# Moving projection tiles behind the block inversion, and re-ordering the queues beside it, in a two-block mixer kernel

## The reference

```python
h = rms_norm(x, pre_norm_w)
qkv, z, b_logit, a_logit = split(h @ w_in)
qkv = silu(causal_depthwise_conv(qkv, conv_w))        # 4 taps
q, k, v = split(qkv)                                  # 8 key heads, 16 value heads of 128
# per value head, in chunks: strictly lower A, (I + A)^-1 applied to v and k
a_mat = where(strict, (k * beta) @ k.T * decay, 0)
u = solve(I + a_mat, v * beta); w = solve(I + a_mat, k * beta * exp(g))
# scan over the chunks, state S
v_new = u - w @ S; o = q_dec @ S + qk @ v_new; S = S * sd + k_dec.T @ v_new
y = (rms_norm(o, norm_w) * silu(z)) @ w_out
...
# memory: the rows of mem are normed by themselves before the key and value projections
kv = rms_norm_2(mem, mem_norm_kv)
```

## Time and profile before

| | |
|---|---|
| median of 3 runs | 1812.25 us (1811.49 to 1813.73) |
| the profiled execution | 1811.49 us, span 1809.7 us |
| mean granted TensorE clock | 0.999 of full speed |
| TensorE busy | 1781.1 us, 98% |
| VectorE busy | 993.0 us, 55% |
| ScalarE busy | 721.1 us, 40% |
| GpSimd busy | 140.6 us, 8% |
| HBM traffic | 86 GB/s over the span |

### The profile page before, as it was taken

One profiled execution on the slowest core, in us unless ns is written; L12 is line 12 of the kernel. 1 busy time (PEld: TensorE's weight loads), 2 busy tenths in 40 slices (PEclk: granted clock), 3 DMA queues, 4 the chain that ended last, 5 costly groups with the idle time before them and its releaser, 6 DMA issues.

```text
span 1809.7 us, 26548 instructions
## 1 busy us (share of the span) xinstructions
PE 1781.1 (98%) x10563; PEld 1438.3 (79%) x10563; DVE 993.0 (55%) x1669; ACT 721.1 (40%) x1381; POOL 140.6 (8%) x108
## 2 busy tenths in 40 slices
PE   8999999999999999999999999999999999999998
PEld 6788888887887888888888777478876778888887
DVE  4645656466537544444443656744333687778434
ACT  5644656457445221111234623754123532223323
POOL 1113031221002000000000001610000100000000
PEclk9999999999999999999999999999999999999999
DMA  6422222122334322333223351023222222332221
GB/s 193 84 61 70 61 63 63 54 71 61 109 102 108 113 93 93 98 104 99 94 93 94 91 117 47 24 70 116 94 70 93 70 93 95 107 99 93 93 76 64
DMA packets 183183, 158.18 MB, mean 87 GB/s; under 512 B 36977, under 2 KB 179886, under 8 KB 183050
## 3 DMA queue, kind: packets, MB, share of 16 engines
q1 hardware_dynamic: 172672, 152.88, 27.6%
q0 software_dynamic: 1248, 3.19, 1.2%
q10 hardware_dynamic: 9163, 0.72, 0.4%
HBM read 152.77 MB, written 3.73 MB: 86 GB/s over the span
## 4 chain that ended last, share of the span: by engine, by line
PE 91%; DVE 4%; ACT 3%; issue 1%; DMA 1%; SPq 0%; POOL 0%; ACTq 0%; DVEq 0%
PE bank L740 13%; PE bank L742 13%; PE bank L741 13%; PE bank L841 5%; PE bank L842 5%; PE bank L843 5%; PE bank L940 4%; PE bank L942 4%; PE bank L941 4%; PE bank L730 4%; PE bank L1067 1%; PE bank L1078 1%; PE bank L1134 1%; PE bank L1089 1%; PE bank L1333 1%
## 5 line engine op out<-in xcount | busy, mean ns | idle before, releaser
L1520 ACT ACTIVATE w_hi<-ring 128x2048 fp32r<-128x2048 f32 x122 | 233.8, 1917 | 535.4 <-PE bank L742 376.3
L740 PE MATMUL bank<-h_hi,w_hi 128*128 128x512 f32 x1024 | 400.4, 391 | 2.2 <-DVE w_lo L2130 2.0
L742 PE MATMUL bank<-h_hi,w_lo 128*128 128x512 f32 x1024 | 398.5, 389 | 0.0
L741 PE MATMUL bank<-h_lo,w_hi 128*128 128x512 f32 x1024 | 398.4, 389 | 0.0
L2130 DVE TENSOR_TENSOR w_lo<-ring,w_hi 128x2048 fp32r<-128x2048 f32 x105 | 240.4, 2289 | 246.4 <-ACT w_hi L1520 246.4
L740 PEld LDWEIGHTS bank<-h_hi,w_hi 128*128 128x128 f32 x1024 | 192.2, 188 | 45.1 <-issue 3.8
L742 PEld LDWEIGHTS bank<-h_hi,w_lo 128*128 128x128 f32 x1024 | 192.2, 188 | 40.3
L741 PEld LDWEIGHTS bank<-h_lo,w_hi 128*128 128x128 f32 x1024 | 192.3, 188 | 39.9 <-issue 0.5
L841 PE MATMUL bank<-h_hi,w_hi 128*128 128x512 f32 x432 | 170.6, 395 | 1.8 <-DVE arena L2823 1.0
L843 PE MATMUL bank<-h_hi,w_lo 128*128 128x512 f32 x432 | 168.2, 389 | 0.0
L842 PE MATMUL bank<-h_lo,w_hi 128*128 128x512 f32 x432 | 168.2, 389 | 0.0
(11 more groups left out here) (441 smaller groups left out, 2508.6 us busy)
## 6 DMA issues: line engine op xcount, KB each, us to landing
ring<-in_sc_w_in SPq DMA_DIRECT2D x32, 1024.0 KB, 5.4
ring<-in_gdn_w_in SPq DMA_DIRECT2D x24, 1024.0 KB, 5.4
ring<-in_w_up SPq DMA_DIRECT2D x22, 1024.0 KB, 5.1
ring<-in_gdn_w_out SPq DMA_DIRECT2D x8, 1024.0 KB, 5.3
ring<-in_sc_w_out SPq DMA_DIRECT2D x8, 1024.0 KB, 5.2
ring<-in_w_down SPq DMA_DIRECT2D x8, 1024.0 KB, 5.3
ring<-in_w_in SPq DMA_DIRECT2D x4, 1024.0 KB, 5.6
ring<-in_w_mk SPq DMA_DIRECT2D x4, 1024.0 KB, 5.1
```

What stands on the lines that cost most here:

```text
L740: pe.matmul(o, a_hi(k), b_hi(k), start=(k == tiles[0]), stop=False)
L741: pe.matmul(o, a_hi(k), b_lo(k), start=False, stop=False)
L742: mm = pe.matmul(o, a_lo(k), b_hi(k), start=False, stop=(k == tiles[-1]))
L1520: act.activation(w_hi[:, plan[n]["pair"], :], ring[:, n % 2, :], ACT.Copy).then_inc(w_hi_ready, 1)
```

## The change

In the delta-rule layer: (a) TensorE's `next_group(1)` and `next_group(3)` ahead of the wait for the blocks go, and the scan's counts rise (first step 5, 5, 4 tiles and not 4, 4, 3; later steps 4, 4, 4 and not 4, 3, 3; in the last step 4 and 4 and not 3 and 3, and then the rest). (b) ScalarE does the squares and roots of the group before ahead of its block copies, and not behind them, and `split_hi(6g+6)` behind the key rows. (c) The low part of slab 6g+6 moves from VectorE, ahead of the inversion, to GpSimd, behind it. (d) `scaled_outs` in groups 1 to 3 moves from ScalarE to VectorE, in the place of that split; VectorE's version is the one that the last group used already. At the seam: (e) SP issues the load of the memory rows behind slab XOUT+1 and not XOUT+3, with the same wait. (f) The statistics of the rows move on ScalarE from ahead of `post_norm` to behind its chunk 0, and (g) their scaling on VectorE from ahead of it to behind the second addition.

```diff
--- before.py
+++ after.py
@@ -661,7 +661,7 @@
                              w_out_2[0, 256 * f:256 * f + 256, o].rearrange("(k d) c -> d k c", d=DH)) for f in range(2)]
                            + [(lambda r: r[:, 1024:SLOT].rearrange("p (k c) -> p k c", c=256),
                                w_out_2[0, 512:D, o].rearrange("(k p) c -> p k c", p=P))])
-                if n == 3:
+                if n == 1:
                     sp.wait_ge(attT_out, NT)
                     sp.dma_start(mem_rows, mem_2[0].rearrange("(t p) c -> p t c", p=P)).then_inc(mem_in, 16)
             load(w_mk_2[0].rearrange("(k p) c -> p k c", p=P)[:, :, 0:256], wide(256))
@@ -1030,6 +1030,12 @@
                     mm.then_inc(vt_done, 1)
                 project(10, range(2, KD))
                 project(11, range(KD))
+                if g:
+                    turn_outs(g - 1, v_of[(g + 1) % 2], banks_read=4 * g)
+                else:
+                    pe.wait_ge(vb_ready, 4)
+                    keep_clock(4, 10)
+                pe.wait_ge(blocks_moved, PER_GROUP * (g + 1))
                 next_tiles = iter([(n, k) for n in range(8) for k in range(KD)])
                 out_sides = iter([(pair, k, side) for pair in range(2) for k in range(KD) for side in range(2)])
 
@@ -1045,16 +1051,6 @@
                                 pe.wait_ge(q_summed, 8 * g + 8)
                             out_tile(VH, 0, pair, k, (side,))
 
-                if ahead:
-                    next_group(1)
-                if g:
-                    turn_outs(g - 1, v_of[(g + 1) % 2], banks_read=4 * g)
-                else:
-                    pe.wait_ge(vb_ready, 4)
-                    keep_clock(4, 10)
-                if ahead:
-                    next_group(3)
-                pe.wait_ge(blocks_moved, PER_GROUP * (g + 1))
                 for lv in range(DEEP):
                     n0 = 4 * (DEEP * g + lv)
                     for h in range(HG):
@@ -1125,7 +1121,7 @@
                             pe.matmul(psum[4 + h][:, 0:P], k_T[h // 2][:, i], state[:, h, :], start=True, stop=True)
                             pe.matmul(psum[4 + h][:, P:2 * P], q_T[h // 2][:, i], state[:, h, :], start=True, stop=True)\
                                 .then_inc(ks_done, 1)
-                    next_group((4 if c < NCH - 1 else 3) if ahead else 1)
+                    next_group((4 if c else 5) if ahead else 1)
                     for h in range(HG):
                         if c:
                             pe.wait_ge(resid_ready, HG * ((NCH - 1) * g + c - 1) + h + 1)
@@ -1133,14 +1129,14 @@
                             pe.wait_ge(y_ready, 4 * (DEEP * (g + 1) - 1) + h + 1)
                         pe.matmul(psum[4 + h][:, 0:P], Y_T[:, h, i], resid[:, h, :] if c else v_T[:, h, i], start=True, stop=True)\
                             .then_inc(vn_done, 1)
-                    next_group((3 if c else 4) if ahead else 1)
+                    next_group((4 if c else 5) if ahead else 1)
                     for h in range(HG):
                         pe.wait_ge(vn_ready, n0 + h + 1)
                         if c < NCH - 1:
                             pe.matmul(psum[4 + h][:, P:2 * P], k_rows[:, h // 2, i], v_dec[:, h, :], start=True, stop=True)
                         pe.matmul(psum[4 + h][:, 2 * P:3 * P], QK_T[:, h, i], v_new[:, h, :], start=True, stop=True)\
                             .then_inc(su_done, 1)
-                    next_group(64 if c == NCH - 1 else 3 if ahead else 2)
+                    next_group(64 if c == NCH - 1 else 4 if ahead else 2)
             turn_outs(GROUPS - 1, v_T)
 
             def x_tiles_back(parts):
@@ -1714,15 +1710,6 @@
                 own.settle()
                 act.activation(ssq[:, 1, :], ssq[:, 1, :], ACT.Exp, scale=-0.5).then_inc(l2_rms, 1)
 
-            def scaled_outs(g, v_T):
-
-                act.wait_ge(l2_rms, 2 * g + 2)
-                for h in range(HG):
-                    for t in range(NT):
-                        rows = v_T[:, h, t * P:(t + 1) * P]
-                        ins = act.activation(rows, rows, ACT.Copy, scale=ssq[:, 1, 4 * h + t:4 * h + t + 1])
-                    ins.then_inc(ssq_ready, 1)
-
             def query_sums(g, j):
                 act.wait_ge(q_turned, 2 * g + j + 1)
                 for t in range(NT):
@@ -1759,20 +1746,17 @@
                         ins = act.activation(decay(g, h)[:, t * P:(t + 1) * P], psum[4 + h][:, t * P:(t + 1) * P],
                                              ACT.Exp, bias=decay_bias(g)[:, t, h:h + 1])
                     ins.then_inc(decay_ready, 1)
+                if g:
+                    out_squares(g - 1, v_of[(g + 1) % 2], (NT - 1,))
+                    out_roots(g - 1)
                 for b in rows_of_scalar:
                     r = slice(BLK * b, BLK * b + BLK)
                     act.wait_ge(a_ready, HG * (g + 1))
                     act.dma_start(block_view(blocks_d, b), diagonal[0][r, :, r]).then_inc(blocks_moved, 16)
-                if g:
-                    out_squares(g - 1, v_of[(g + 1) % 2], (NT - 1,))
-                split_hi(6 * g + 6)
-                if g:
-                    out_roots(g - 1)
                 for j in range(2):
                     act.wait_ge(kr_done, 2 * g + j + 1)
                     act.activation(k_rows[:, j, :], psum[4 + 2 * j][:, :], ACT.Copy).then_inc(kr_ready, 1)
-                if g:
-                    scaled_outs(g - 1, v_of[(g + 1) % 2])
+                split_hi(6 * g + 6)
                 for n in range(8, 11):
                     projected(g, n)
                 for b in rows_of_scalar:
@@ -2006,16 +1990,16 @@
                     if what == "c":
                         out_columns(n)
 
-            act.wait_ge(mem_in, 16)
-            for t in range(MT):
-                own.did(act.activation(mem_junk, mem_rows[:, t, :], ACT.Square, accum_out=small[:, 1 + t:2 + t]))
-                own.settle()
-            own.did(act.activation(small[:, 1:3], small[:, 1:3], ACT.Ln, bias=eps, scale=1.0 / D))
-            own.settle()
-            act.activation(small[:, 1:3], small[:, 1:3], ACT.Exp, scale=-0.5).then_inc(mem_rstd, 1)
-
             def mem_beside(k):
 
+                if k == 0:
+                    act.wait_ge(mem_in, 16)
+                    for t in range(MT):
+                        own.did(act.activation(mem_junk, mem_rows[:, t, :], ACT.Square, accum_out=small[:, 1 + t:2 + t]))
+                        own.settle()
+                    own.did(act.activation(small[:, 1:3], small[:, 1:3], ACT.Ln, bias=eps, scale=1.0 / D))
+                    own.settle()
+                    act.activation(small[:, 1:3], small[:, 1:3], ACT.Exp, scale=-0.5).then_inc(mem_rstd, 1)
                 if 3 <= k < 7:
                     for j in (2 * k - 6, 2 * k - 5):
                         act.wait_ge(mem_turned, j + 1)
@@ -2426,7 +2410,7 @@
                     dve.tensor_tensor(QK_T[:, h, :], kq[:, h // 2, :], decay(g, h), ALU.mult).then_inc(decay_used, 1)
                 if g:
                     out_means(g - 1)
-                split_lo(6 * g + 6)
+                    scaled_outs(g - 1, v_of[(g + 1) % 2])
                 invert_blocks(g)
                 for h in range(HG):
                     dve.wait_ge(vt_done, 4 * g + turn_order.index(h) + 1)
@@ -2769,9 +2753,11 @@
                     if (what, s, n) == ("s", len(steps) - 1, 3):
                         shares(s, n)
 
-            dve.wait_ge(mem_rstd, 1)
-            own.did(dve.tensor_scalar(mem_rows[:, 0, :], mem_rows[:, 0, :], small[:, 1:2], None, ALU.mult))
-            dve.tensor_scalar(mem_rows[:, 1, :], mem_rows[:, 1, :], small[:, 2:3], None, ALU.mult).then_inc(mem_scaled, 1)
+            def mem_scale(k):
+                if k == 1:
+                    dve.wait_ge(mem_rstd, 1)
+                    own.did(dve.tensor_scalar(mem_rows[:, 0, :], mem_rows[:, 0, :], small[:, 1:2], None, ALU.mult))
+                    dve.tensor_scalar(mem_rows[:, 1, :], mem_rows[:, 1, :], small[:, 2:3], None, ALU.mult).then_inc(mem_scaled, 1)
 
             def split_q0(k):
                 if k == 5:
@@ -2779,7 +2765,7 @@
                     dve.tensor_tensor(w_lo[:, Q0["pair"], :], q0_slab, w_hi[:, Q0["pair"], :].bitcast(F32), ALU.subtract)\
                         .then_inc(split_ready, 1)
 
-            post_norm(between=split_q0, ahead=lambda pair: split_lo(XOUT + 2 + pair) if pair < 2 else None)
+            post_norm(beside=mem_scale, between=split_q0, ahead=lambda pair: split_lo(XOUT + 2 + pair) if pair < 2 else None)
             split_lo(MEM0 + 4)
             norm_ready()
             q0 = plan[MEM0 + 3]["end"] - 2
@@ -2877,6 +2863,7 @@
                     pool.wait_ge(vn_done, HG * NCH * g)
                 pool.memset(Y_T, 0.0).then_inc(y_cleared, 1)
                 pool.wait_ge(inverted, g + 1)
+                split_lo(6 * g + 6)
                 split_lo(6 * g + 7)
                 if g + 1 < GROUPS:
```

## The result

The changed kernel took 1830.71 us (median of 4 runs, 1828.8 to 1833.78), the kernel before, beside it on the same chip, 1812.47: a ratio of 1.0102, 95% interval 1.0089 to 1.0115. It is 18.2 us slower, and the forecast was 8.6. Its profiled execution took 1827.32 us with a span of 1825.5 and a mean granted clock of 0.996; ten runs of it, that one among them, had a mean clock of 0.9935.

The account below looks back on a forecast made before the run. TensorE, busy 98% of the span, bounds the kernel, so only its stalls count. Blocks +3.7, memory rows' stall +3.2 and clock +1.7 sum to +8.6 us; forecast 1820.9 us, its own range 1817 to 1823.

Parts of the forecast that it names:

- clock behind L1063: After the new stalls before L1067, some 2.3 us each: no clock drop, 0, with 5.1 us as upper bound.
- wait at the memory rows: At L1407 TensorE stands from 1216.15 to 1219.4 for VectorE's late scaling: +3.2 us, bounds 2.6 and 4.7.
- clock behind the memory rows: Behind the stall at L1407 the granted clock drops as it did behind L730: +1.7 us, bounds 0 and 1.7.
- signs of being right: L1067 waits 2 us or more, block copies 3 us late, last scan matmuls 1.05, L1407 waits 3 with a dip.
- the block chain's terms: Late inverted blocks at L1067, moved tiles and scan gain counted: -0.8, +1.7, +1.7, +1.1 in groups 0 to 3, +3.7 us.
- Part 1: Four tiles moved behind L1067: 2.7 us less cover there, 1.0 us won in the scan's last step, groups 0 to 2.
- Part 3: The split on GpSimd behind the inversion, 4.58 us against VectorE's 2.29: costs 0, and doesn't hold VectorE.
- Part 4: Memory rows at the seam: load not earlier, statistics and scaling late, TensorE stalls +3.2 us, clock drop behind it +1.7.
- the shorter chain: Rival at ScalarE's first block copy, groups 1 to 3: not late, L1067 waits for nothing, 1813 or 1808; chance 0.10.
- hidden memory edit: Rival at the memory rows: TensorE doesn't meet the late scaling, only the blocks' +3.7 stays, 1816; chance 0.10.
- GpSimd holding VectorE: Rival at VectorE's scaling of v: starts 4.6 us late in every group, +13 on the forecast, 1834; chance 0.06.
- The clock rival: Rival at L1067: the clock drops there too, one to three more drops of 1.7 us, 1822.6 to 1826.0; chance 0.14.

Follow-up runs that it names:

- e10: The changed kernel with the memory edit undone: 1826.35 us, 1.0072 of the kernel before.
- e11: The changed kernel with the memory edit undone and idle matmuls (8, 12, 7) in the stalls before L1063 of groups 1 to 3: 1821.74 us, ratio 1.0041.
- e9: The kernel before with only the four tiles moved behind L1067: 1817.65 us, ratio 1.0029.
- e13: The changed kernel as it is, measured again in a later session: 1828.37 us, 1.0089 of the kernel before.
- e3: The changed kernel with ScalarE's block copies again ahead of the squares and roots: 1818.47 us, 1.0028 of the kernel before.
- e8: The kernel before with the tiles moved and the split on GpSimd, but ScalarE's order, scaled outputs and memory rows as before: 1812.12 us, ratio 0.9998.
- e4: The changed kernel with the four tiles again ahead of L1063 and the old counts in the scan: 1834.27 us, 1.012 of the kernel before.
- e7: The kernel before with only ScalarE's squares and roots of the group before put ahead of its block copies: 1818.15 us, ratio 1.0028.
- e1: The kernel before with the memory edit alone: 1815.82 us, ratio 1.0019.
- e5: The changed kernel with idle matmuls (8, 12, 7) in the stalls before L1063 of groups 1 to 3: 1828.54 us, 1.0087 of the kernel before.
- e6: The changed kernel with tiles ahead of L1063, old scan counts, and the split on VectorE between scaled outputs and inversion: 1825.37 us, 1.0068 of the kernel before.
- e12: The kernel before with four tiles in each scan step's first two slots and the split on GpSimd in the last group alone: 1809.78 us, ratio 0.9979.

## Why the prediction was wrong

It had the mechanism, every new wait in its place and the sign, and was wrong in size. Against the profiled executions (1811.49 and 1827.32, +15.8) the terms are:

| term | predicted | measured |
|---|---|---|
| L1003 to L1067, groups 0, 1, 2, 3 | -2.5, 0, 0, +1.1 | -1.8, +1.0, +1.7, +1.7 |
| L1067 to the next L1003, groups 0 to 2, without dips | +1.7 each | +1.5, +1.3, +1.4 |
| scan of group 3 | 0 | +0.9 |
| clock behind L1063 | 0 | +3.4 |
| wait at the memory rows | +3.2 | +3.0 |
| clock behind the memory rows | +1.7 | 0 |
| a clock dip before the first L1003 | 0 | +1.5 |
| sum | +8.6 | +15.6 |

In an unprofiled run 2.4 us more are lost; the ten runs' mean clock of 0.9935 against the profiled 0.996 puts them on the clock, but not on one place.

**The first step that failed is the clock behind the new L1067 stalls.** The prediction priced it at 0, since stalls of 2.3 us were "nearer to 2.4", the wait at L885 that drew no dip. It was 3.4 us in the profile, and e10 against e11 puts it at 4.6 to 5.6 us in ordinary runs, around the upper bound of 5.1 that the prediction had kept for a rival of 0.14. The row that decided was one draw. In the changed kernel's own profile the same wait at L885, 18 us into the execution and touched by no edit, drew a dip; its timeline and the windows behind it:

```profile
17.81 0.47 PE L885 MATMUL bank<-h_hi,w_hi 128*128 128x512 f32 x1 [2.48 <-DVE h_lo L2241]
```

```profile
18.00:20.00 2.00, 2.00 (x7) 1.37 (x7) 2.00 (x4) 2.00 (x4) 2.00 (x1) 0.69 0.70 170
20.00:22.00 2.00, 2.00 (x6) 1.58 (x5) 2.00 (x4) 2.00 (x3) 0.88 (x1) 0.50 0.06 7
22.00:24.00 2.00, 2.00 (x10) 1.61 (x9) 1.52 (x2) 0.95 (x2) 0.00 (x0) 0.95 0.92 245
```

It is the 1.5 us before the first L1003 in the table, and it came in five of the fourteen profiles. Behind waits of 2.0 us and more at L1063 a dip came in seven of twelve (behind 2.04 us, and not behind 2.23), behind those of under 1.7 us in none; at the memory rows, 3.0 us and once 3.6, in two of seven; at L730, 2.8 us, in thirteen of fourteen. So neither the length alone nor one row says whether it comes, and the memory rows, to which the prediction gave the whole 1.7, are where it came least: of the signs of being right, the dip behind L1407 is the one that is missing.

What makes the places differ stays open. The rival's "idle of 2.3 us after sparse transposes" fits L1063, and L730 too, as its rows in the changed kernel show:

```profile
1385.85 0.60 PE L1449 MATMUL bank<-masks,arena 128*128 128x128 f32 x4
1386.85 0.41 PE L1449 MATMUL bank<-masks,arena 128*128 128x128 f32 x2 [0.40 <-ACT arena L2055]
1390.08 2.98 PE L730 MATMUL bank<-arena 128*128 128x512 f32 x4 [2.82 <-ACT arena L2055]
```

Ahead of the memory rows' wait stand dense projection matmuls. But L885, which drew a dip in five of fourteen, stands behind sixteen transposes (L871). So that is a fit of a few places and no test of it; shown is only that activity in the stall takes the dip away. The page TensorE: Matmul & The Clock Gate of the Trainium skill, section "Why this matters for your kernels", warns of longer idle gaps between matmul bursts, since the clock falls back behind them. Here the length didn't sort the cases: a wait of 2.04 us at L1063 drew a dip (e9), and of the seven at the memory rows, 3.0 us and more, five drew none.

**The second is the size of the block chain's terms, 4.0 us in all, nearly all of it ahead of L1067.** That ScalarE's copies come 3.1 us late was right (16.76 us after L1003 against 13.75: 3.0). But the landing of L558 was put at 2.0 us, and the blocks came 3.0, 2.1 and 2.9 us after its issue in groups 1 to 3, so the inversion is 1.8, 1.3 and 1.6 us late and not 1.1; and the way back from L564 was put at 5.23, the one value that the profile before shows bare, and was 6.06, 5.55, 6.75 and 5.27. The transfer of group 3, the shortest, was used for all. e9 points the same way from the other side: with nothing late it leaves the blocks of groups 0 and 1 some 0.3 and 0.5 us of slack. The spread lies in the last leg: from L564 to SP's issue at L569 it took 1.73 to 1.75 us in each group, from there to L1063 4.31, 3.82, 5.02 and 3.53. Why group 2 is longer than groups 1 and 3 in all runs of this order (6.75; 6.42 in e13, 6.51 in e10, 6.90 in e11; but 5.25 in e3) stays open.

**Part 1** was right where it spoke of the scan: 1.05 us again, and 1.3 us back per group rather than 1.0. **Part 3** was right: VectorE's scaling of v, from 213.69, took 2.48 us beside GpSimd's split (2.47 before; GpSimd's row in group 1 stands below this paragraph), and tiles with GpSimd's split cost nothing (e8). That agrees with the Trainium skill (GPSIMD Engine Reference, section 1, Specifications), which has the SBUF interface shared with VectorE's instructions of two SBUF inputs; these read a PSUM bank. What it left out is the tie that e4 laid bare. **Part 4** was right in its stall: VectorE's adding, twice scaling, and TensorE 0.06 us behind.

```profile
213.86 4.54 POOL L2849 TENSOR_TENSOR w_lo<-ring,w_hi 128x2048 fp32r<-128x2048 f32 x1 [35.18 <-DVE arena L2376]
```

The change's gains and losses don't add up singly. Tiles and GpSimd's split cost nothing (e8), and roots first alone cost 5.1 us (e7), nearly all at L1029, where the changed kernel doesn't wait. But in the changed kernel the same order of ScalarE costs 11 to 13 (e3 against it). Of those, 8.8 us are later starts of L1063 in groups 1 to 3 (the table: 2.75, 3.62 and 2.45), and the two dips of the profile, 3.4 us, are about the rest. That the blocks' lateness costs more there because VectorE's split and, in groups 1 and 2, the tiles no longer cover it is my reading; no run takes that cover away by itself with the copies late.

The rivals: the shorter chain and the hidden memory edit are ruled out by the rows and by e1, GpSimd holding VectorE by the 2.48 us and by e8. The clock rival was true, at its top, and with the terms of the block chain beside it.

## What to carry to other kernels

A stall of TensorE of 2 us or more has two prices here, its length and with some chance a clock dip of 1.7 us: count the second by its share over many stalls, not by one row, or fill the stall with idle matmuls, which gave back 4.6 us in one pair of kernels (e10 and e11) and 2.7 us or nothing in another (e5). A DMA issue that others wait for goes ahead of work that waits for another engine, on every queue; and before taking cover away in front of a round trip, take its length as the spread over the groups, not as the shortest row. Where a change moves readers and producer together, undoing one of them measures neither.

## What the runs showed of the hardware

- The granted clock fell to 0.50 behind a stall and came back by itself, mostly with 1.7 us lost, in some executions and not in others at the same place: three, two and one times at L1063 in three profiles of code that is the same there (e10, the changed kernel, e13). The same kernel's runs spread with it (1833.65 us at a mean clock of 0.991, 1827.32 at 0.996).
- Seven to twelve idle matmuls of 128x512 in the stall kept the clock at 1.00 although TensorE still waited for the same blocks (e11: 0.9978 over its runs, against 0.9940 in e10 without them).
- The two DMA trips of 16x16 blocks vary by over a microsecond between groups of one execution: in the changed kernel 1.9 to 3.0 us from L558 to the inversion and 5.3 to 6.8 from L564 to L1063, and 8.6 in group 0 of e6 and e12, where ScalarE's four issues took 3.0 us and not 1.86.
